# Hybrid diffusion step: the keys of the chosen ranks are formed rank by rank on VectorE and GpSimd, and the one-hot blocks are shared out anew

## The reference

```python
def peer(h, w_pq, sub_keys, expert_u, expert_v):
    qh = (t @ w_pq).reshape(T, PEER_HEADS, 2, D_HALF)             # 8 heads, 2 halves of 128
    scores = jnp.einsum('thpd,hpkd->thpk', qh, sub_keys)          # 128 keys per half
    s_top, i_top = lax.top_k(scores, PEER_TOPK)                   # 16 ranks: score and key
    cand = s_top[:, :, 0, :, None] + s_top[:, :, 1, None, :]
    cand_idx = i_top[:, :, 0, :, None] * N_KEYS + i_top[:, :, 1, None, :]
    best, pos = lax.top_k(cand.reshape(T, PEER_HEADS, -1), PEER_TOPK)
    idx = jnp.take_along_axis(cand_idx.reshape(T, PEER_HEADS, -1), pos, axis=-1)
    gate = jax.nn.softmax(best, axis=-1)
    ...
    act = jax.nn.gelu(jnp.einsum('td,thkd->thk', tb, expert_u[ib]))
    return jnp.einsum('thk,thkd->td', gb * act, expert_v[ib])
```

## Time and profile before

| | before |
|---|---|
| median of three runs | 3799.74 us |
| lowest and highest run | 3797.67, 3799.96 us |
| profiled execution: its own time | 3798.86 us |
| its span | 3797.1 us |
| TensorE busy | 3605.6 us |
| VectorE busy | 2667.4 us |
| GpSimd busy | 1894.8 us |
| ScalarE busy | 628.9 us |

### The profile page before, as it was taken

How to read it: one execution, slowest core, us unless ns; L and a number is a source line. 1 busy time by engine, 2 the same in 40 slices (tenths; PEclk the granted TensorE clock), 3 DMA queues, 4 the chain that set the end, 5 groups by cost and what they waited for, 6 DMA issues and landing times. The chain is left out here.

```text
span 3797.1 us, 45352 instructions
## 1 busy us (share of the span) xinstructions
PE 3605.6 (95%) x15346; PEld 2481.3 (65%) x15346; DVE 2667.4 (70%) x5705; ACT 628.9 (17%) x1536; POOL 1894.8 (50%) x1593
## 2 busy tenths in 40 slices
PE   7999997899999999999989999879999999999998
PEld 3445576667666766666655456776776667666666
DVE  4424598887878667666665356898878777676667
ACT  3212216510000000000021231281000000000000
POOL 0011029866676566666501100597566755666663
PEclk8999999999999999999999999999999999999999
DMA  9711206999999999999951022199999999999997
GB/s 395 293 58 53 100 25 112 275 386 401 403 408 408 356 408 401 408 408 408 382 200 40 28 76 77 40 162 368 378 406 406 408 390 380 408 404 408 408 408 280
DMA packets 496520, 1116.54 MB, mean 294 GB/s; under 512 B 201360, under 2 KB 240400, under 8 KB 495104
## 3 DMA queue, kind: packets, MB, share of 16 engines
q0 software_dynamic: 175104, 637.61, 42.5%
q1 hardware_dynamic: 316768, 463.63, 35.5%
q10 hardware_dynamic: 4512, 13.76, 1.0%
HBM read 1068.68 MB, written 46.12 MB: 294 GB/s over the span
## 5 line engine op out<-in xcount | busy, mean ns | idle before, releaser
L1501 PE MATMUL ps<-big,y_nat 128*128 128x336 f32 x4096 | 1216.6, 450 | 54.6 <-DMA y_nat<-in_peer_ut 46.8
L1501 PEld LDWEIGHTS ps<-big,y_nat 128*128 128x128 f32 x4096 | 761.6, 190 | 438.8 <-issue 100.4
L2102 POOL DMA_INDIRECT big<-in_peer_u,gates_area x608 | 769.4, 1265 | 460.4 <-DVE kn_area L1888 286.6
L2113 POOL DMA_INDIRECT big<-in_peer_v,gates_area x608 | 690.9, 1136 | 416.0 <-DVE big L1906 269.6
L1906 DVE SCALAR_TENSOR_TENSOR big<-big,kn_area 128x1024 f32<-128x1024 f32 x608 | 785.4, 1292 | 7.0 <-DVE big L1906 0.5
L1888 DVE CUSTOM_DVE_ANT_0 big<-big,y_nat 128x1024 f32<-128x1024 f32 x608 | 739.7, 1223 | 1.3
L1616 ACT ACTIVATE gates_area<-ps 128x336 f32<-128x336 f32 x256 | 115.2, 450 | 2034.7 <-PE ps L1501 2034.7
L1514 PEld LDWEIGHTS ps<-gates_area,y_nat 128*128 128x128 f32 x2048 | 363.7, 190 | 61.2 <-issue 61.2
L1514 PEld LDWEIGHTS ps<-gates_area,big 128*128 128x128 f32 x2048 | 363.7, 190 | 61.2 <-issue 61.2
L1514 PE MATMUL ps<-gates_area,big 128*128 128x208 f32 x2048 | 381.0, 339 | 0.0
L1514 PE MATMUL ps<-gates_area,y_nat 128*128 128x208 f32 x2048 | 381.0, 339 | 0.0
(11 more groups left out here) (294 smaller groups left out, 3388.8 us busy)
## 6 DMA issues: line engine op xcount, KB each, us to landing
y_nat<-in_peer_ut SPq DMA_DIRECT2D x256, 512.0 KB, 8.4
y_nat<-in_peer_v SPq DMA_DIRECT2D x128, 512.0 KB, 6.7
big<-in_peer_v SPq DMA_DIRECT2D x128, 512.0 KB
big<-in_w_mod SPq DMA_DIRECT2D x24, 2048.0 KB, 13.4
expert_gates<-big SPq DMA_DIRECT2D x8, 4096.0 KB, 22.2
gates_area<-expert_gates SPq DMA_DIRECT2D x128, 136.0 KB, 9.5
kn_area<-expert_gates SPq DMA_DIRECT2D x128, 136.0 KB, 9.9
big<-in_w_in SPq DMA_DIRECT2D x8, 2048.0 KB, 15.6
```

Of the source, the lines that this page charges most:

```text
L1501: last = pe.matmul(ps[:, 6 + par, 0:NX], u_s[par][:, k, :], h_t[:, k, X0:ND], start=(k == 0), stop=(k == KD - 1))
L2102: pool.indirect_dma_start(out=u_ring[:, k % USLOTS, :], out_offset=None, in_=io["peer_u"][:, :], in_offset=bass.IndirectOffsetOnAxis(ap=ro ...
L2113: pool.indirect_dma_start(out=v_ring[:, k % VSLOTS, :], out_offset=None, in_=io["peer_v"][:, :], in_offset=bass.IndirectOffsetOnAxis(ap=ro ...
```

## The change

The keys of ranks are no longer formed in 12 units that go from VectorE to GpSimd and back. One instruction now handles one rank for all 384 slots of one half (`dense_ranks`): it compares the ranks with that rank's number and multiplies with the key at that rank. Ranks 0 to 10 (`RANKS_V` = 11) are VectorE's, 11 to 15 GpSimd's, and each engine's products are summed over its own ranks by VectorE and added. The row half's ranks 8 to 10 and 0 to 7 go in two pieces, since they lie in different memory.

`choices(0)` stands before step `CHOICE_AT` = 14 of the 17 steps of the other tiles' queries instead of after them, in another PSUM bank. The exponential stands after ScalarE's step 5. The first three one-hot groups are scaled in ScalarE's steps 14 to 16, and the groups' PSUM pairs are 1 and 2 instead of 0 and 1. Of 32 tokens, ScalarE scales 20 (was 18), GpSimd makes 6 (was 7), VectorE 6 (was 7). The copy `sc_4` moves behind the seventh group's scaling. VectorE and GpSimd no longer wait for all scores before the groups.

```diff
+RANKS_V = 11
+CHOICE_AT, CHOICE_BANK = 14, (4, 6, 7)
+PREBUILT = 2 * PH + 1 - CHOICE_AT
-BY_SCALAR = (4, 5, 4, 5)
-BY_POOL = (2, 2, 2, 1)
+BY_SCALAR = (5, 5, 5, 5)
+BY_POOL = (2, 1, 2, 1)
...
                     for g in range(2 * PH + 1):
+                        if g == CHOICE_AT:
+                            choices(0)
...
-                    pe.wait_ge(s_top, PH)
-                    pe.wait_ge(s_sbe, 2 * PH)
-                    pe.wait_ge(s_rk, 1)
-                    choices(0)
...
+                        if g == 5:
+                            act.wait_ge(s_b7, 1)
+                            act.activation(exp_gate[:, 0:DENSE, :], gate_xa, ACT.Exp).then_inc(s_e7, 1)
+                        if g >= CHOICE_AT:
+                            scale_hots(g - CHOICE_AT)
+                    for n in range(PREBUILT - 1):
+                        evacuate(n)
+                    for n in range(PREBUILT, GROUPS):
+                        i, g = (n + SKIPPED) // 16, (n + SKIPPED) % 16
+                        if g == 10 and i + 1 < DENSE:
+                            choices(i + 1)
+                        scale_hots(n)
+                        if n == HOTS + 3:
+                            act.activation(sc_4, ...).then_inc(s_sbe, 1)
+                        evacuate(n - 1)
...
+                    dve.engine_nop().then_inc(s_rd, 1)
+                    def dense_ranks(x, rank, eq, r0, r1):
+                        key, v = keys_by_head(x), eq.rearrange("p (s k a) -> p s k a", k=TOPK, a=r1 - r0)
+                        for r in range(r0, r1):
+                            lane.do(dve.scalar_tensor_tensor(
+                                out=v[:, :, :, r - r0], in0=rank.rearrange("p t (h k) -> p (t h) k", k=TOPK), scalar=float(r),
+                                in1=key[:, :, r:r + 1].broadcast_to([P, DENSE * PH, TOPK]), op0=ALU.is_equal, op1=ALU.mult))
+                        lane.settle()
...
+                    dense_ranks(0, rowf_a, eq_tail, TOPK // 2, RANKS_V)
+                    key_sum(eq_tail, RANKS_V - TOPK // 2, dense_ids[0])
                     dve.wait_ge(s_qs, 16 * (1 + NG))
-                    for u in range(4 * DENSE):
-                        compare(u, eq_a, (rowf_a, colf_a))
-                        if u >= 2:
-                            resolve(u - 2, u - 1, 0, eq_a)
+                    dense_ranks(0, rowf_a, eq_a, 0, TOPK // 2)
+                    add_key_sum(0, eq_a, TOPK // 2)
                     softmax(0, DENSE, 1)
+                    dve.wait_ge(s_q, 3 * PH)
+                    dense_ranks(1, colf_a, eq_v, 0, RANKS_V)
+                    key_sum(eq_v, RANKS_V, dense_ids[1])
+                    for x in range(2):
+                        dve.wait_ge(s_kp, x + 1)
+                        add_key_sum(x, eq_p[x], TOPK - RANKS_V)
                     expert_rows(0, colf_a[:, 0, :])
...
-                    for u in range(4 * DENSE):
-                        keys_of_ranks(u, u + 1, eq_a, top_ifa)
-                    pool.wait_ge(s_s, 4 * PH)
+                    pool.wait_ge(s_rd, 1)
+                    for x, rank in enumerate((rowf_a, colf_a)):
+                        if x == 1:
+                            pool.wait_ge(s_q, 3 * PH)
+                        for a in range(RANKS_V, TOPK):
+                            pool.tensor_scalar(v[:, :, :, a - RANKS_V], rank..., float(a), 1.0, ALU.is_equal, ALU.mult).then_inc(s_eq, 1)
+                        pool.wait_ge(s_eq, (TOPK - RANKS_V) * (x + 1))
+                        pool.tensor_tensor(v, v, keys_by_head(x)[:, :, RANKS_V:TOPK]..., ALU.mult).then_inc(s_kp, 1)
```

More of the change, by code:

```diff
@@ L232, in build @@
         NB_ = len(GATHERED)
-        q_r = carve(big, 21504, 2, ND)
+        q_r, q_g = carve(big, 21504, 2, ND), carve(kn_area, 2048, 2, len(GATHERED) * P)
         cut_a = carve(big, 22272, 2, ND)
@@ L1453, in _, with choices @@
                             natural_rows(g // 2 - 2)
+                    def choices(i):
+                        if i == 0:
+                            pe.wait_ge(s_top, PH)
+                            pe.wait_ge(s_rk, 1)
+                        else:
+                            pe.wait_ge(s_sbe, 2 * PH)
+                        for q, src in enumerate((exp_i1, exp_i2, exp_gate)):
+                            last = pe.transpose(ps[:, CHOICE_BANK[i], q * P:(q + 1) * P], src[:, i, :], ident[:, :])
+                        last.then_inc(s_ft, 1)
                     pe.wait_ge(s_nat, NG + 1)
                     for g in range(2 * PH + 1):
+                        if g == CHOICE_AT:
+                            choices(0)
                         if g < 2 * PH:
@@ L1467, in _ @@
                             for t in range(NG):
-                                last = pe.matmul(ps[:, 6 + f % 2, t * P:(t + 1) * P], q_r[:, f % 2, t * P:(t + 1) * P],
+                                last = pe.matmul(ps[:, 6 + f % 2, t * P:(t + 1) * P], q_g[:, f % 2, t * P:(t + 1) * P],
                                                  keys_t[:, f, :], start=True, stop=True)
                             last.then_inc(s_s, 1)
-                    pe.wait_ge(s_top, PH)
-                    pe.wait_ge(s_sbe, 2 * PH)
-                    def choices(i):
-                        for q, src in enumerate((exp_i1, exp_i2, exp_gate)):
-                            last = pe.transpose(ps[:, 6 + i % 2, q * P:(q + 1) * P], src[:, i, :], ident[:, :])
-                        last.then_inc(s_ft, 1)
-                    pe.wait_ge(s_rk, 1)
-                    choices(0)
                     for n in range(GROUPS):
@@ L1491, in _ @@
                         for tt in range(OCT):
-                            last = pe.matmul(pair(n % 2)[:, tt * P:(tt + 1) * P], hot2[:, n % HOTS, tt, :], hot1[:, n % HOTS, tt, :],
+                            last = pe.matmul(pair(1 + n % 2)[:, tt * P:(tt + 1) * P], hot2[:, n % HOTS, tt, :], hot1[:, n % HOTS, tt, :],
                                              start=True, stop=True)
@@ L1593, in _ @@
                             choices(i + 1)
[L1594 to L1600 removed]
+                        scale_hots(n)
+                        if n == HOTS + 3:
+                            act.activation(sc_4, sc_b[:, 0, :, :].rearrange("p (k a) b -> p k (a b)", a=2), ACT.Copy).then_inc(s_sbe, 1)
+                        evacuate(n - 1)
                     evacuate(GROUPS - 1)
@@ new lines, in key_sum, with add_key_sum @@
+                    def key_sum(eq, ranks, dst):
+                        lane.do(dve.tensor_reduce(dst.rearrange("p t s -> p (t s)"), eq.rearrange("p (s a) -> p s a", a=ranks), AX.X, ALU.add))
+                        lane.settle()
+                    def add_key_sum(x, eq, ranks):
+                        key_sum(eq, ranks, key_tail)
+                        lane.do(dve.tensor_tensor(dense_ids[x], dense_ids[x], key_tail, ALU.add))
+                        lane.settle()
+                    dense_ids = exp_i1[:, 0:DENSE, :], exp_i2[:, 0:DENSE, :]
```

77 lines of the change are left out of this document (31 added, 46 removed).

## The result

The changed kernel takes 3806.34 us in the median of 12 runs (3801.72 to 3809.61), the kernel before 3797.94 us in 12 runs on the same chips (3789.1 to 3810.57). The ratio is 1.0019 [1.001, 1.0027]: slower by 0.19%, some 7 us, where 24 us faster was forecast. The profiled execution took 3809.61 us with a span of 3807.8; it is the slowest of the twelve.

A forecast was written before the change was run, and what follows sets the result against it. It took TensorE's gap before the choices and the groups' pace, with stores just below, as bounds. 10.9 us to the first full store plus 2.1 behind it made 13.0 a layer, 26.0 in all: 3774 us, range 3765 to 3787.

The forecast's parts named there:

- When the ranks are ready: Rank stage ahead of the choices: ready at 2444 (2456.1 before), between VectorE alone at 2438.0 and full collision at 2447.1.
- full exclusion: Rival: ranks ready at 2447 to 2449, stall at step 14 of 6 to 8 us, 3780 to 3784 us; chance 0.15.
- so I charge nothing: VectorE's rank instructions, writing 3, 8 or 11 words apart: no extra time, at most 0.07 us each, 1.5 us.
- Its case in the prediction: Skill's price for VectorE's single-word writes: an estimated 5.7 us longer, ranks ready near 2450, 3786 us.
- GpSimd's comparison: GpSimd's 128x384 rank comparison: 1.30 us each, bounds 0.8 and 3.3; its rank work done at 2431.3.
- The slower rival: Choices come later than before, needing GpSimd comparisons of 3.5 us; at 4.0 each, 3809 us; chance 0.10.
- The stall at step 14: TensorE reaches step 14 at 2440.99 and waits for the ranks until 2444, 3 us.
- the gap: Kernel before: TensorE, between its last scores and the choices, waited 6.6 us for VectorE; first groups then ran at clock 0.50.
- The pace of the groups: One-hot groups up to the first full store: 2.40 us each, ScalarE tightest; GpSimd's one-hots 1.50 each.
- the groups keep their pace: Rival: GpSimd's one-hots get in as rarely as before, stores stay 20.9 us apart, 3778 us; chance 0.02.
- From the first full store to the stream: Stores bind at 20 us each: last lands 82.2 us after the first is issued (84.3 before), worth 2.1 us.
- The signs that the prediction gave for being wrong: Last landing over 84 us, wait over 8, one-hots over 1.9; GpSimd's comparison over 2, VectorE's instruction every 0.7.

The follow-up runs named there:

- e6: Changed kernel with VectorE's rank work held back until GpSimd has made its first product; one execution took 3833.76 us.
- e5: Changed kernel with VectorE's products laid out rank by rank, written in a row and summed with a stride; 3806.59 us, ratio to before 1.0019.
- e3: Changed kernel with one one-hot block of every 8 on GpSimd, five on ScalarE and two on VectorE; 3782.42 us, ratio to before 0.9962.
- e9: e3 with the choices ahead of step 16 instead of 14; 3777.12 us, ratio to before 0.9932.
- e1: Changed kernel with the old shares of one-hots (ScalarE 4,5,4,5, GpSimd 2,2,2,1 of each 8); 3801.91 us, ratio to before 1.0012.
- e8: Changed kernel with rank-by-rank products, 13 column-half ranks on VectorE and 3 on GpSimd, one GpSimd block a group; 3784.27 us, ratio 0.9963.

## Why the prediction was wrong, step by step

**When the ranks are ready.** Forecast 2444, by the clock of before; measured 2451.4 with a first query 4.2 us later, so 2447.2, in the place of the rival "full exclusion". Only half by that rival's way. VectorE's own stretch was 37.0 us instead of 27.8, of which the forecast had allowed 6.0 for taking turns with GpSimd. Its sums were right (13.6 us by the rows, 13.7 forecast). The 22 rank instructions took 17.1 us in place of 10.6, and the first addition 2.7 instead of 0.5, since it met GpSimd's first product. Of the 6.5 us on the instructions some 2.0 are turn-taking: 1.2 in the column half (e6), and 0.8 in the row half, where three instructions that met a comparison held the next off by 0.25 to 0.3 us more than their neighbours. So turn-taking cost VectorE about 4.2 us, less than the 6.0 allowed, and the writes' distance 4.5, for which nothing was allowed.

The step that failed is "so I charge nothing" for strided writes. I judged by instructions of 64 columns, 16 words apart, at 0.14, where a small price per element can't be seen. e5 measured 0.22 us for 384 elements. The 0.48 between starts was right: in e5, where the writes lie in a row, it is 0.47.

The Trainium skill's page "Vector Engine (DVE) Microarchitecture Reference", section "Measured stream behaviour on trn2", gives about 0.65 cycle an element more where each element hops to another region, an estimated 0.26 us here, and says that small steps cost more than large ones. The runs show 0.22 at 8 and 11 words, so no more than its figure for large hops. Its case in the prediction (ready near 2450, 3786) was 2.8 us late, where my 2444 was 3.2 early; it named the cause of half the delay, and I set it aside for a row of another size.

**GpSimd's comparison.** Forecast 1.30 from a line through two other shapes, measured 1.94 alone and 2.25 beside VectorE; the product, 4.0 forecast, 4.05. GpSimd's 31 us still end 6 us ahead of VectorE, so this miss of 10 us cost no more than the turn-taking above. The slower rival named 3.5 us as its point; that was not reached, and the choices did come earlier than before. That rival's number, 3809, is close to the outcome by luck: the loss has another cause.

**The stall at step 14.** Forecast 3.0, measured 6.2. The queries behind it were charged 8.7 us and took 11.1, for the block behind the idle time ran near the lower of the clock's two levels, 1.2 of 2.4 GHz: the windows of the kernel after (us, PE, PEld, DVE, ACT, POOL, PEclk, DMA share, GB/s) give a granted clock of 1.00 ahead of it and 0.56 behind it.

```profile
2441.00:2445.00 4.00, 4.00 (x24) 3.59 (x23) 4.00 (x1) 0.81 (x3) 3.92 (x2) 1.00 0.00 0
2452.00:2458.00 6.00, 6.00 (x18) 4.85 (x18) 5.02 (x8) 0.49 (x1) 4.95 (x3) 0.56 0.00 1
```

The prediction let the stall take the gap's place but not its clock. First group: 163.8 forecast, 169.2 measured; first full store 190.7 and 197.3.

**The pace of the groups.** This is the step that cost most: "I take 2.40 a group". ScalarE does take 2.37, as forecast. GpSimd's 6 blocks per four groups were given 1.50 each, 9.0 us, under ScalarE's 9.6; they took 6 x 1.87 = 11.2. Beside that GpSimd waited 10.4 us a layer for buffers, for which there was no term. The 1.50 was a mean over blocks stretched by VectorE and blocks that passed at its short pauses, and the mix came from the even pattern of the old shares. With the new ones a long block took 2.4 us instead of some 2.05, and a third of the blocks were short instead of two fifths. The bound stood in the rows, a maximum of 2.45; it was used for the range of the comparison, not for the one-hots. The prediction's "there VectorE never paused" is wrong too: it paused 28 times a layer, and that is where the 0.79 came from. Even the rival "the groups keep their pace" took the old pace to be the worst; nothing in the list let it fall.

**From the first full store to the stream.** Forecast 82.2 us until the last landing, measured 93.7: 11.5 of the miss. Stores of 20 us were right, as e3's first layer and e9 show (82.9 and 83.6 there), but they weren't the bound: the groups were, by GpSimd's blocks and TensorE's waits. The stream's first matmul came 2.2 us behind the last landing, where it was 1.1 ahead of it before, as TensorE multiplies its last groups until 2585.6.

In sum for the second layer, counted from the first query: choices 3.4 late, the queries behind them 2.1, the groups up to the first full store 1.1, the stores 11.5, the stream behind them 3.3. Together 21.4, from 13.0 earlier to 8.4 later. The signs that the prediction gave for being wrong all but came: the last store landed 93.7 us after the first, the one-hots took 1.87 on average (1.9 named), a rank's instruction took over 0.7, GpSimd's comparison over 2. They were in the text and not in the chances.

**What stays open.** In e1 the groups start 5 us earlier than before and the stream at most 1.7. GpSimd's total is 4.5 us longer there, and its first groups come with VectorE's long stops, which fits the same cause, but no run tells it apart from the stores' order. That uneven groups cost the rest of the 8 us in the kernel after is read from its chain; no run changes the pattern alone. Nor is it shown whether GpSimd's block waits for VectorE's two inputs to SBUF or for something else that L1889 and L1892 have and L1897 has not; it was not tried with other operands.

## What to carry to other kernels

A duration of an instruction that shares a resource is a result of the schedule, not a constant. Before changing shares, split its durations into those that ran alone and those that met the neighbour, and ask which of them remain when the neighbour's pauses move: here their sum grew from 8 to 28 us a layer, and fewer short blocks passed. Price a new access pattern by a row of the same size, or measure it by itself, and don't take a row of few elements for proof that nothing is charged. A stall moved ahead of other matmuls brings its clock along. Charge the first block behind it at up to the lower level: 6.16 us in the kernel after and 4.65 in e1 for what took 3.62 before.

## What the runs showed of the hardware

- A 128x128 one-hot of GpSimd's takes 0.79 us at VectorE's pauses and 2.44 to 2.48 without exception (84 of 84 in e3) beside a VectorE that runs two-input instructions of 0.81 and 1.21 us and two single-input ones in a round of 2.44. VectorE's instructions keep their durations, the 1024-wide one 1.21 in both, and the first of the pair also where a short one-hot still runs beside it.
- With a GpSimd product of two inputs it is VectorE that stands: the addition that met one took 2.74 us instead of 0.56, and a rank's instruction in e8 2.51 instead of 0.55. Beside GpSimd's comparisons about one VectorE instruction for each comparison is held up, by 0.25 to 0.3 us.
- VectorE instructions with a scalar and two inputs over 384 columns start every 0.47 us when they write in a row (e5), and alone every 0.67 when they write 11 words apart (e6). Beside GpSimd's comparisons the means are 0.56 and 0.78 to 0.79 (0.69 for three of them at 3 apart). A sum over 3072 elements takes 3.35 us when it reads in a row, and 5.58 when it reads 384 words apart.
- GpSimd's comparison with two fixed scalars over 384 columns, writing 5 words apart, takes 1.94 us alone, against 1.81 for the 640 columns of another line.
- After 6.2 us without a matmul the next 16 took 6.15 us in the kernel after and in e3, not 3.62, and 4.65 in e1. After 2.8 us (e9) two groups took 5.50, not 3.74, at a granted clock of 0.69; after waits of 2.84 us in the kernel after it was sometimes 5.44 and sometimes 3.81.
